# Weight halves as contiguous runs of DRAM in a streamed-weight fp32 network

## The reference

```python
def first_block(x, ...):
    h = layer_norm(x, ln_in_g, ln_in_b)
    for l in range(2):
        mix = mixer_sublayer(h, ..., w_in[l], ..., w_out[l])
        h = layer_norm(DEEPNORM_ALPHA * h + mix, ln1_g[l], ln1_b[l])
        ffn = grouped_moe(h, router_w, router_bias, exp_w_gate[l], exp_w_up[l], exp_w_down[l])
        h = layer_norm(DEEPNORM_ALPHA * h + ffn, ln2_g[l], ln2_b[l])
    return h

def grouped_moe(h, ...):
    ...
    for e in range(16):                       # every expert's weights are read
        a = silu(h @ w_gate[e]) * (h @ w_up[e])
        y = y + dense_gates[:, e:e + 1] * (a @ w_down[e])
    return y

def swiglu(h, wi, wo):                        # four of these in the second block, inner width 2816
    gate, up = jnp.split(h @ wi, 2, axis=-1)
    return (silu(gate) * up) @ wo
```

## Time and profile before

| | us |
|---|---|
| median of 3 runs | 2271.04 |
| lowest and highest run | 2266.41, 2272.28 |
| profiled execution, its own time | 2278.06 |
| span of the profiled execution | 2276.2 |
| PE busy | 2143.1 |
| DVE busy | 1549.2 |
| ACT busy | 1246.3 |

### The profile page before, as it was taken

How to read it: one execution, slowest core, us unless ns; L and a number is a source line. 1 busy time by engine, 2 the same in 40 slices (tenths; PEclk the granted TensorE clock), 3 DMA queues, 4 the chain that set the end, 5 groups by cost and what they waited for, 6 DMA issues and landing times.

```text
span 2276.2 us, 32506 instructions
## 1 busy us (share of the span) xinstructions
PE 2143.1 (94%) x12234; PEld 1857.6 (82%) x12234; DVE 1549.2 (68%) x2172; ACT 1246.3 (55%) x1985; POOL 50.0 (2%) x64
## 2 busy tenths in 40 slices
PE   6988999998988999998999999899999999899999
PEld 5767878776777787776999898789999998778998
DVE  6457989996457899986655657556566566655665
ACT  4353777773454777774544565554445445454443
POOL 0000000000000000001000000000000000000000
PEclk8898999998998999999999999999999999899999
DMA  6222999993123999994455562525555556134553
GB/s 231 69 75 95 330 335 359 357 356 127 63 75 133 334 348 353 353 346 153 159 194 179 166 200 69 175 97 191 185 186 176 194 180 208 60 130 130 180 185 118
DMA packets 124215, 446.81 MB, mean 196 GB/s; under 512 B 14320, under 2 KB 15472, under 8 KB 123120
## 3 DMA queue, kind: packets, MB, share of 16 engines
q1 hardware_dynamic: 124048, 444.61, 56.7%
HBM read 443.51 MB, written 1.05 MB: 195 GB/s over the span
## 4 chain that ended last, share of the span: by engine, by line
PE 48%; DVE 2%; ACT 2%; issue 1%; DMA 0%; POOL 0%; SPq 0%; DVEq 0%; ACTq 0%
PE bank L670 8%; PE bank L671 8%; PE bank L672 8%; PE bank L628 4%; PE bank L1067 4%; PE bank L1068 4%; PE bank L1069 4%; PE bank L629 4%; PE bank L630 3%; PE bank L2597 1%; PE bank L2579 1%; PE bank L940 0%; DVE lo L591 0%; DMA scr<-in_alibi 0%; ACT scr L3240 0%
## 5 line engine op out<-in xcount | busy, mean ns | idle before, releaser
L591 DVE TENSOR_TENSOR lo<-stage,hi 128x1024 fp32r<-128x1024 f32 (+1 forms) x834 | 974.0, 1204 | 271.5 <-ACT hi L579 240.2
L579 ACT ACTIVATE hi<-stage 128x1024 fp32r<-128x1024 f32 (+1 forms) x834 | 842.7, 1043 | 289.5 <-DMA stage<-in_exp 101.9
L670 PE MATMUL bank<-thi,hi 128*128 128x256 f32 x1504 | 427.5, 284 | 5.3 <-DVE tlo L746 3.3
L671 PE MATMUL bank<-tlo,hi 128*128 128x256 f32 x1504 | 426.3, 283 | 0.0
L672 PE MATMUL bank<-thi,lo 128*128 128x256 f32 x1504 | 426.3, 283 | 0.0
L670 PEld LDWEIGHTS bank<-thi,hi 128*128 128x128 f32 x1504 | 289.1, 192 | 8.0 <-issue 6.5
L671 PEld LDWEIGHTS bank<-tlo,hi 128*128 128x128 f32 x1504 | 289.2, 192 | 1.4
L672 PEld LDWEIGHTS bank<-thi,lo 128*128 128x128 f32 x1504 | 289.2, 192 | 0.0
L628 PE MATMUL bank<-hi,thi 128*128 128x512 f32 (+3 forms) x656 | 260.1, 396 | 20.1 <-DVE tlo L746 7.9
L629 PE MATMUL bank<-lo,thi 128*128 128x512 f32 (+3 forms) x656 | 253.4, 386 | 0.0
L630 PE MATMUL bank<-hi,tlo 128*128 128x512 f32 (+3 forms) x656 | 253.1, 386 | 0.0
(11 more groups left out here) (369 smaller groups left out, 2759.1 us busy)
## 6 DMA issues: line engine op xcount, KB each, us to landing
stage<-in_exp SPq DMA_DIRECT2D x384, 512.0 KB, 6.0
stage<-in_ffn SPq DMA_DIRECT2D x264, 512.0 KB, 5.0
stage<-in_wi_a SPq DMA_DIRECT2D x16, 512.0 KB, 6.8
stage<-in_wi_b SPq DMA_DIRECT2D x16, 512.0 KB, 4.8
stage<-in_mem_wkv SPq DMA_DIRECT2D x16, 512.0 KB, 6.2
stage<-in_xwq SPq DMA_DIRECT2D x16, 512.0 KB, 4.7
stage<-in_xwo SPq DMA_DIRECT2D x16, 512.0 KB, 5.0
stage<-in_ssd_xbc SPq DMA_DIRECT2D x12, 512.0 KB, 5.2
```

Of the source, the lines that this page charges most:

```text
L579: a.activation(self.hi[i % NR][:, x:y], self.stage[(2 * i + p) % (2 * NS)][:, :y - x], ACT.Copy).then_inc(*c.tick(("hi", i, p), sem="hi"))
L591: v.tensor_tensor(self.lo[i % NR][:, x:y], self.stage[(2 * i + p) % (2 * NS)][:, :y - x], self.hi[i % NR][:, x:y].bitcast(F32), ALU.subtra ...
L670: t.matmul(out, hi[:, ws], self.thi[:, xs], start=(k == 0), stop=False)
L671: t.matmul(out, hi[:, ws], self.tlo[:, xs], start=False, stop=False)
```

## The change

Each chunk is stored in DRAM as two blocks, one after the other: first the left half of the columns for all 128 partitions, then the right half. `load` reads a half as one run of `128 * n / 2` floats. Before, it read n/2 floats of each partition's n, and skipped the other n/2. The number of DMAs, their order, their waits, their sizes and their destinations in SBUF are the same, and so is every other instruction.

```diff
@@ pack_weights
-    return {n: np.concatenate(out[n]) for n, _ in STREAM}
+    return {n: np.concatenate([half for chunk in out[n] for half in halves(chunk)]) for n, _ in STREAM}
+
+
+def halves(chunk):
+
+    x = chunk.reshape(128, -1)
+    n = x.shape[1] // 2
+    return x[:, :n].reshape(-1), x[:, n:].reshape(-1)
@@ load
         name, at, n = self.chunks[i]
-        src = self.d[name][at:at + 128 * n].rearrange("(p c) -> p c", p=128)
         for p, (x, y) in enumerate(((0, n // 2), (n // 2, n))):
+            src = self.d[name][at + 128 * x:at + 128 * y].rearrange("(p c) -> p c", p=128)
             if i >= NS:
                 for w in c.need(("hi", i - NS, p), ("lo", i - NS, p)):
                     s.wait_ge(*w)
             b = (2 * i + p) % (2 * NS)
-            s.dma_start(self.stage[b][:, :y - x], src[:, x:y]).then_inc(*c.tick(("ld", i, p), sem=f"ld{b}", by=16))
+            s.dma_start(self.stage[b][:, :y - x], src).then_inc(*c.tick(("ld", i, p), sem=f"ld{b}", by=16))
```

## The result

The changed kernel takes 2255.69 us (median of 6 runs, 2251.03 to 2256.85) against 2273.14 us (median of 6 runs of the kernel before), a ratio of 0.9915 with a 95% interval of 0.9894 to 0.9936. It is faster by 0.85%, where the forecast was no change. The profiled execution took 2252.88 us, with a span of 2251.1 us against 2276.2 us: 25.1 us less.

The account below looks back on a forecast made before the run. The prediction took PE as the bound outside the expert stages, and DMA and PE together within them. All terms were zero, leaving the profiled 2278.06 us, carried over to the runs' median as 2271 us; range 2254 to 2286.

Parts of the forecast that it names:

- the faster case: Expert stages: DRAM serves whole runs better, gain limited by PE; 13 us taken, 2258 us (2251 to 2264), chance 0.22.
- the reading of the pitch: Loads of halves: strided ones reached 420 GB/s at the kernel's start, so the 8 KiB pitch costs nothing; term zero.
- cover for a late issue: SP's queue: halves in flight hide each load's 0.1 us later start; taken as zero, 38 us if cover were gone.
- the transfers' need: Expert stages: a chunk of 1.049 MB needs 2.87 us of DMA at 366 GB/s, against 2.70 us of PE.
- Bound by DMA and PE together: Expert stages, 286 and 279 us: DMA engines busy 96%, PE 278.70 and 272.85 us, the two nearly level.
- The limit of the gain: Both expert stages shrink by PE's idle time at most: 13.4 us, plus 6.6 us for gaps, 20 us at best.
- The signs: Faster case in expert stages: ACT's waits well under 101.9 us, with a rate above 380 GB/s or lower DMA share.
- SP's issue of 425 ns: SP's queue: changed loads take about 425 ns instead of 328, 81 us more over 834 loads, hidden; cost zero.
- Same packets, same order: Loads of halves: 834 before and after, same order, waits, sizes and 4 KB packets; cost zero.
- Outside the expert stages zero: Elsewhere weights arrive early and PE sets the time; zero, with ±0.6 us at the start.
- The slower rival: Expert stages: contiguous runs fetched at the `mem` window's 327 GB/s, 2322 us; half the penalty, 2290 us, likeliest; chance 0.12.
- The warning about pitches: Expert stages: if 8 KiB cost the skill page's 3%, up to 8 us for each stage; left to the faster case.

Follow-up runs that it names:

- e4: Kernel of loads and splits alone (no matmuls), with the splits left out: 1.261 us for a half at 8 KiB pitch, 1.250 us at 4 KiB.
- e2: Against the kernel before, all chunks but those of the expert layers laid out in contiguous halves: 2269.96 us, ratio 0.9976.

## Why the prediction was wrong

The prediction named the place and the limit of the faster case rightly (the price only roughly: 13 us, measured 17.5), and gave that case 0.22. The measured 2255.69 us lies in the range of 2254 to 2286, near its lower end, but the forecast was no change and the kernel became faster.

**The step that failed** is the reading of the pitch: "a pitch that held the rate at 366 could not have let it reach 420". The 420 GB/s of the earlier trace rows were measured while six halves and other loads stood in the queue. With a full queue a later landing costs no rate; e4 shows 410 GB/s at 8 KiB and at 4 KiB alike. So the sum's term for the pitch, put at zero, was in fact 19.0 us in the two stages. In the expert stages the same later landing is part of a round through six buffers, and there it does cost. I compared rates where I should have compared landing times under like conditions. The trace of before held nothing that was quite alike, but it held the round: landing of 6.0 us in the stage, two splits of 2.3 us, six buffers. From that it was to be seen that a change of the landing time comes back as up to a sixth of it for every half: 384 x 0.7 / 6 = 45 us by this estimate, if nothing else had held the stages up. PE did: 19.0 us came through, about what the prediction had worked out as PE's limit. I used a landing time, 5.4 us over all loads, only to argue that "some three and a half are in flight", as cover for a late issue. In the stages it is 6.0 / 1.46 = 4.1 in flight and 2.3 / 1.46 = 1.6 with the splits, 5.7 of six buffers in use: no spare depth. What was called the transfers' need, 2.87 us for a chunk at 366 GB/s, was the pace of this round and not what the transfer engines can do; with the same halves and seven buffers they moved 409 GB/s.

**Bound by DMA and PE together**: right in that the loads and PE held each other level, wrong in taking the loads' side for a limit of the transfer engines. PE lacked 12.9 us before and lacks 3.7 us after.

**The limit of the gain**: "20 us at the very best" in the two stages; measured 19.0. The two terms were 13.4 us of PE not busy (9.2 were regained) and 6.6 us hidden behind the modelled ends (9.8, of which some 3.4 are the clock, which the prediction did not price). That the sum comes so near to 19.0 is in part luck: 4.2 us less of the first term and 3.2 more of the second. I then took 13 for no reason of the profile's. That a modest gain in rate "gives only part of this" was wrong too: the rate rose by 3.5 and 4.7% (341 to 353, 344 to 360 GB/s), and nearly everything was had.

**The signs**: of those named for the faster rival one came, ACT's waits for expert halves at 19.7 us against 101.9. The rate above 380 GB/s or the lower DMA share did not.

**SP's issue of 425 ns**: wrong. It stayed at 328 ns. The 424 ns of `mem` have another cause, which was not looked for. The step carried no time, so nothing hung on it.

**Same packets, same order**: right, 124215 before and after.

**Outside the expert stages zero**: the second block is unchanged, as said; its halves land 0.7 us sooner and nobody waits for them. Zero was wrong for the first block outside the stages, whose start I had bounded at 0.6 us: e2 gains 0.24% (0.08 to 0.40%) in all. About 2 us stand before 48 us in its profile, most of them perhaps PE's clock. In the slices the first has a DMA digit of 6 and 231 GB/s, far above its neighbours, and I passed over it.

**The slower rival**: contiguous loads at 327 GB/s, read off the window of `mem`, didn't come. That window says nothing about contiguous loads; 353 to 366 GB/s in the stages do.

**The warning about pitches.** The Trainium skill, in "DMA: Bandwidth & Descriptors", section "Latency and other measured facts", says that row pitches at large powers of two lose rate and that tiles should be padded or made contiguous. The direction is what the runs show, and I gave it no part in the sum, since its smallest pitch is 512 KiB and no row showed such a one. The size is not what they show: here it is 8 KiB that costs, 16 and 32 KiB cost 1% or nothing in a stream, and 64 B of padding is enough with six buffers, where the page found that 192 B did not help its 4 MiB pitch.

## What to carry to other kernels

Where weights come through a few buffers that are also read by other engines, work out the round of one buffer (landing, each reader, release) and divide it by the number of buffers: if that is the time of one piece, landing time is throughput, as it was here at a busy share of 95%. How much of it can be had is set by the next limit, here PE. A rate measured while the queue is full says nothing about such a loop. And before a layout is rebuilt, try a few bytes of padding in each row: here 64 B did the same as the new layout.

## What was not expected of the hardware

Rows of 4 KiB that lie exactly 8 KiB apart in DRAM make a 512 KiB load land later by 0.7 us (5.9 against 5.2 us in a stream with splits, 4.3 against 3.6 in bursts of two with and without splits). In the stream 6, 12 and 32 KiB, and 8 KiB + 64 B, don't, and 16 KiB hardly does (5.3 us). With splits and six buffers that is 7 to 9% of the time for a half; with seven or more buffers it is 1% or less. A DMA share of 95 to 97% did not mean that the transfers were at their limit: the share is 0.95 in the first expert stage before and after, at 341 and 353 GB/s.
